# Last attention of a two-block transformer kernel: outputs formed transposed in one PSUM bank, gates and softmax sums multiplied into the weights on GpSimd

## What is computed

```python
q = rmsnorm(proj[..., :1024].reshape(b, s, 16, 64), q_norm)
gate = sigmoid(proj[..., 1024:])                       # 3 gates per head
o_cmp = softmax(q @ k_cmp.T) @ v_cmp                   # 15 compressed keys
o_sel = softmax(masked(q @ k_sel.T)) @ v_sel
o_win = softmax(masked(q @ k_win.T)) @ v_win
out = gate0 * o_cmp + gate1 * o_sel + gate2 * o_win
h = h + out.reshape(b, s, 1024) @ w_o
```

## Time and profile before

| | |
|---|---|
| median of three runs | 1619.47 us (1617.98 to 1620.32) |
| the profiled execution, its own time | 1619.05 us |
| its span, first to last instruction | 1616.0 us |
| PE busy | 1600.5 us, 99% of the span |
| DVE busy | 1033.2 us, 64% |
| ACT busy | 802.4 us, 50% |
| POOL busy | 36.8 us, 2% |
| DMA | 291.21 MB, mean 180 GB/s |
| PE clock granted, mean | 1.000 |
| the chain that ended last | PE 91%, DVE 5%, ACT 2% |

### The profile page before, as it was taken

The page is one execution under the profiler, slowest core; times in us unless marked ns, Lnnn a source line. Parts: engine busy times, 40 slices in busy tenths (PEclk is TensorE's granted clock), DMA queues, the critical chain, the costliest instruction groups (busy, mean ns, idle before and its releaser), DMA issues.

```text
span 1616.0 us, 21201 instructions
## 1 busy us (share of the span) xinstructions
PE 1600.5 (99%) x8796; PEld 1375.2 (85%) x8796; DVE 1033.2 (64%) x1223; ACT 802.4 (50%) x1091; POOL 36.8 (2%) x53
## 2 busy tenths in 40 slices
PE   8999999999999999999999999999999999999999
PEld 6888898877888888888899888889888887888887
DVE  5666556887766747666457666557666557766662
ACT  5555254765355534554344555446555445555551
POOL 0000000000000000000000000001000011000000
PEclk9999999999999999999999999999999999999999
DMA  9665574435476546555464665557565551056652
GB/s 289 186 228 184 170 261 137 144 117 176 141 224 212 218 147 217 183 198 201 162 219 156 204 191 196 196 173 247 168 193 200 187 195 53 11 172 195 197 182 78
DMA packets 226559, 291.21 MB, mean 180 GB/s; under 512 B 10596, under 2 KB 203808, under 8 KB 226336
## 3 DMA queue, kind: packets, MB, share of 16 engines
q1 hardware_dynamic: 226464, 289.87, 54.6%
HBM read 288.78 MB, written 1.05 MB: 179 GB/s over the span
## 4 chain that ended last, share of the span: by engine, by line
PE 91%; DVE 5%; ACT 2%; SPq 1%; issue 1%; DMA 1%; POOL 0%; DVEq 0%
PE bank L2003 24%; PE bank L2008 12%; PE bank L1813 9%; PE bank L1818 9%; PE bank L1822 9%; PE bank L1901 5%; PE bank L1888 5%; PE bank L1893 5%; PE bank L1862 2%; PE bank L1869 2%; DVE w_lo L1125 2%; PE bank L1864 2%; PE bank L2380 1%; PE bank L1789 1%; DMA raw<-in_ffn_w_up_dram 1%
## 5 line engine op out<-in xcount | busy, mean ns | idle before, releaser
L1125 DVE TENSOR_TENSOR w_lo<-raw,w_hi 128x2048 fp32r<-128x2048 f32 (+1 forms) x267 | 599.7, 2271 | 172.9 <-ACT w_hi L710 171.9
L710 ACT ACTIVATE w_hi<-raw 128x2048 fp32r<-128x2048 f32 (+1 forms) x267 | 506.6, 1904 | 167.4 <-DMA raw<-in_ffn_w_down_dram 93.4
L2003 PE MATMUL bank<-xT,w_hi 128*128 128x512 f32 x1664 | 397.3, 391 | 0.0
L2003 PEld LDWEIGHTS bank<-xT,w_hi 128*128 128x128 f32 x1664 | 306.1, 188 | 59.5
L2008 PEld LDWEIGHTS bank<-xT,w_lo 128*128 128x128 f32 x1664 | 213.3, 191 | 8.1
L2008 PE MATMUL bank<-xT,w_lo 128*128 128x256 f32 x1664 | 215.9, 283 | 0.0
L1072 ACT ACTIVATE silu<-bank 128x256 f32<-128x256 f32 x104 | 34.2, 381 | 215.9 <-PE bank L2008 215.9
L1818 PE MATMUL bank<-w_hi,hT_lo 128*128 128x512 f32 x528 | 134.9, 390 | 0.0
L1813 PE MATMUL bank<-w_hi,hT_hi 128*128 128x512 f32 x528 | 133.8, 389 | 0.0
L1822 PE MATMUL bank<-w_lo,hT_hi 128*128 128x512 f32 x528 | 133.7, 389 | 0.0
L1888 PE MATMUL bank<-w_hi,xT 128*128 128x512 f32 (+2 forms) x456 | 119.3, 392 | 0.0
(11 more groups left out here) (290 smaller groups left out, 1584.3 us busy)
## 6 DMA issues: line engine op xcount, KB each, us to landing
raw<-in_ffn_w_gate_up_dram SPq DMA_DIRECT2D x176, 512.0 KB, 4.8
raw<-in_ffn_w_down_dram SPq DMA_DIRECT2D x132, 512.0 KB, 4.0
raw<-in_w_in_dram SPq DMA_DIRECT2D x44, 512.0 KB, 4.9
raw<-in_ffn_w_gate_dram SPq DMA_DIRECT2D x43, 512.0 KB, 4.0
raw<-in_ffn_w_up_dram SPq DMA_DIRECT2D x43, 512.0 KB, 5.0
raw<-in_conv_w_in_dram SPq DMA_DIRECT2D x24, 512.0 KB, 4.6
raw<-in_kv_w_dram SPq DMA_DIRECT2D x12, 512.0 KB, 4.2
raw<-in_w_out_dram SPq DMA_DIRECT2D x8, 512.0 KB, 3.9
```

The source lines that it names most:

```text
L710: nc.scalar.activation(w_hi[:, slot, 0:width], raw[:, slot, 0:width], ACT.Copy).then_inc(high_ready, 1)
L1125: nc.vector.tensor_tensor(w_lo[:, slot, 0:width], raw[:, slot, 0:width], w_hi[:, slot, 0:width].bitcast(F32), ALU.subtract).then_inc(low_r ...
L2003: nc.tensor.matmul(o[:], hi[:, c, at], x, start=kh == 0 and c == 0, stop=False, skip_group_check=True)
```

## The change

**Scores.** A unit's banks are divided otherwise (`HEADS_AT`): bank 0 holds two tt = 1 heads, banks 1 and 2 one tt = 1 head and two tt = 0 heads each. The four 256-column matmuls come first, then the four of 128 columns, always one of each partition half in turn. Each bank signals for itself: `sel_scored`, `sel_least`, `sel_exped`, `sel_weighed`, `sel_scaled` and `selT_psum` count three per unit. The queries carry the factor -1/8, so minima replace maxima and the small negation goes.

**Coefficients.** `weigh` takes the banks one by one: three reciprocals and three products per unit in place of one each. GpSimd first copies the gates into a table by unit (`unit_gate`, eight copies), and then multiplies each head's weights in `sel_p` by its coefficient, eight tensor_scalar operations per unit. The transposes now wait for that (`sel_scaled`).

**Outputs.** The values are stationary (64 columns wide), the weights move: nine f32 matmuls per unit, of 256 or 128 columns, whose result has the features on partitions. The two heads of a pair write the two partition halves of a bank. The selected, the window and the compressed branch of a chunk add up in one bank (6 or 7 in turn), and ACT and DVE take `xT_hi` and `xT_lo` straight from it (`attended_chunks`). `add_unit`, `add_compressed` and the 16 transposes of `z_sb` go.

**Order.** The first w_o slab is interleaved with the last unit's transposes and outputs (`opening`). On DVE `weigh` moves ahead of the copy for unit 0, and from unit 3 on minima and `weigh` alternate by banks around the split of a weight slab.

```diff
-        SCORES = [[3, 4, 5], [0, 1, 2]]
+        SCORES = [[4, 2, 3], [5, 0, 1]]
+        CMP_TURNED = 7
+        HEADS_AT = [[(1, 0), (1, 3)], [(1, 1), (0, 0), (0, 1)], [(1, 2), (0, 2), (0, 3)]]
-        SCORE_ORDER = [(0, 0), (1, 2), (0, 1), (1, 3), (0, 2), (1, 0), (0, 3), (1, 1)]
+        SCORE_ORDER = [(1, 0), (1, 2), (1, 1), (1, 3), (0, 0), (0, 2), (0, 1), (0, 3)]
```

On GpSimd, behind the query roots:

```diff
+                    pool.wait_ge(branch_gates, 1)
+                    for b in range(3):
+                        for k, (tt, i) in enumerate(HEADS_AT[b]):
...
+                            ins = pool.tensor_copy(to, src[:, :, :, 1:3, i // 2, i % 2])
+                    ins.then_inc(unit_gates, 1)
+                    for w in range(UNITS):
+                        for b in range(3):
+                            pool.wait_ge(sel_weighed, 3 * w + b + 1)
+                            for k, head in enumerate(HEADS_AT[b]):
+                                p, c = sel_p[:, w % 2, b, score_place(*head)[1]], FIRST_AT[b] + k
+                                ins = pool.tensor_scalar(p, p, sel_coef[:, w % 2, c:c + 1], None, ALU.mult)
+                            ins.then_inc(sel_scaled, 1)
```

On ACT:

```diff
+                    for w in range(2, UNITS):
+                        if w + 1 < UNITS:
+                            exponentials(w + 1, range(0, 1))
+                        turned_weights(w)
+                        if w == 2:
+                            compressed_weights(0)
                         if w == 3:
+                            compressed_weights(1)
+                        if w + 1 < UNITS:
+                            exponentials(w + 1, range(1, 3))
+                        if w == 2:
                             split_to(s0 + 7)
-                        transposed_weights(w)
-                    evacuate_input(inputs_before(n) + 1, HALVES_FIRST)
+                        if w >= 3 and w != 5:
+                            attended_chunks({3: 0, 4: 1, 6: 2, 7: 3}[w])
```

On DVE:

```diff
-                    row_maxima(1)
-                    transposed_weights(0)
+                    row_minima(1)
                     weigh(0)
+                    turned_weights(0)
...
                     masked(0)
-                    row_maxima(2)
-                    transposed_weights(1)
+                    row_minima(2)
+                    weigh(1)
                     masked(1)
+                    turned_weights(1)
...
-                    weigh(1)
-                    add_unit(0)
+                    weigh(2)
+                    row_minima(3)
...
                     for w in range(3, UNITS):
...
+                        turned_weights(w)
+                        if w + 1 < UNITS:
+                            weigh(w + 1, range(0, 1))
                         if w <= 5:
                             split_to(s0 + w + 2)
...
+                        if w != 5:
+                            attended_chunks({3: 0, 4: 1, 6: 2, 7: 3}[w])
+                        if w + 1 < UNITS:
+                            weigh(w + 1, range(1, 2))
+                            if w + 2 < UNITS:
+                                row_minima(w + 2, range(0, 1))
+                            weigh(w + 1, range(2, 3))
+                            if w + 2 < UNITS:
+                                row_minima(w + 2, range(1, 3))
```

On PE:

```diff
                     def transpose_weights(w):
-                        pe.wait_ge(sel_exped, w + 1)
                         for b in range(3):
-                            for i in range(4):
...
-                        ins.then_inc(selT_psum, 1)
+                            pe.wait_ge(sel_scaled, 3 * w + b + 1)
+                            for to, i in enumerate(TURNED_FROM[b]):
+                                ins = nc.tensor.transpose(bank[SCORES[w % 2][b]][:, to * P:(to + 1) * P], sel_p[:, w % 2, b, i * P:(i + 1) * P], ident[:])
+                            ins.then_inc(selT_psum, 1)
...
-                        for tt in range(NT):
-                            for r in range(PER_GROUP):
...
-                                    ins = nc.tensor.matmul(o, p, values[:, key_tile, g * HD:(g + 1) * HD], start=key_tile == 0, stop=key_tile == tt)
+                        weighted(0, 0, every, 3)
+                        weighted(1, 0, every, 0)
+                        weighted(0, 1, second, 5)
+                        weighted(1, 1, second, 2)
+                        weighted(2, 0, every, 9)
+                        weighted(3, 0, first, 8)
+                        weighted(3, 0, second, 7)
+                        weighted(2, 1, second, 11)
+                        weighted(3, 1, second, 6).then_inc(sel_out, 1)
...
+                    def opening(part):
+                        pe.wait_ge(xT_ready, first_input + 2)
+                        part(0, [0])
+                        transpose_weights(7)
+                        part(1, [0], between=last_units)
+                        pe.wait_ge(xT_ready, first_input + 4)
+                        part(0, [1], True).then_inc(slab_used, 1)
```

More of the change, by code:

```diff
@@ L1826, in project @@
                 first = slabs - tail(n)
-                for d in range(first):
+                if opening:
+                    opening(part)
+                for d in range(0 if not opening else first, first):
                     ready(d)
@@ L1838, in project @@
                 for tt in range(NT):
-                    for d in range(first, slabs):
+                    for d in range(first + 1 if opening and tt == 0 else first, slabs):
                         between = None
@@ new lines, in outputs @@
+                        every, first, second = slice(0, S), slice(0, P), slice(P, S)
+                        weighted(0, 0, every, 3)
[7 more added lines that the diff above has]
+                        weighted(3, 1, second, 6).then_inc(sel_out, 1)
@@ L2441, in _ @@
[L2441 to L2447 removed]
+                    transpose_weights(4)
```

297 lines of the change are left out of this document (133 added, 164 removed).

## The result

The changed kernel takes 1647.2 us (median of 4 runs, 1645.87 to 1648.97), the kernel before on the same chip 1618.72 (1617.6 to 1620.32): 1.0176 times as long, 95% interval 1.0158 to 1.0193. The forecast was 1622.0 with a range to 1631; it is outside. The profiled execution took 1648.97 us, its span 1647.1. Four executions of the kernels in this document (1758 to 3206 us) were in a slower state of the chip and are left out of all medians.

What follows compares the result with a forecast made beforehand. PE, busy 99% at full clock, was taken as the bound. Four attention stretches and shorter scores summed -0.3 + 8.1 - 2.5 + 0.8 - 4.0 = +2.1 us, plus 1 for `weigh`'s product: 1619.05 + 3 = 1622.0 us, range 1616 to 1631.

Steps and rivals of the forecast that it cites:

- the assumed prices: GpSimd's scaling passes: 0.94 us for bank 0 and 1.19 us each for banks 1 and 2 of a unit.
- the dear passes: Rival: GpSimd's scaling passes take 4 to 4.7 us a unit, giving +6 to +9.5 us; chance 0.17.
- 3.3 us a unit: GpSimd's eight scaling passes of a unit, priced from rows of other operations; bounds 2.8 and 4.7 us.
- full clock: Forecast case: PE's clock stays full, GpSimd 2.8 to 3.8 us a unit, time +0 to +5.5 us; chance 0.50.
- The clock rival: Rival: PE idles about 3 us twice in the attention and its clock falls, +4 to +7 us more; chance 0.23.
- stretch A: Attention from unit 1's scores to the end of unit 1's transposes: 17.7 us for 9.6 before, +8.1.
- B: Attention from there to the end of unit 4's transposes: 24.9 us for 27.4 before, -2.5.
- C: Two rounds of the attention's rhythm: 14.4 us together for 13.6 before, +0.8.
- the ring of C: Chain of `weigh`, GpSimd, transposes, copies, slab split and reduction: 7.0 us one round, 7.2 to 7.4 the second.
- D: Rest of the attention: 7.8 us for 10.9 before plus 0.9 of transposes inside the projection, -4.0.
- 1 us for the small product in `weigh`: DVE's two-input product waits for a GpSimd pass, 0.4 us at most, in about five units: 1 us more.
- scores 1.5: A unit's eight score matmuls, equal sizes side by side: 1.5 us in place of 1.84, 2.7 us saved in all.

Runs made afterwards that it cites:

- the waits filled: Changed kernel with dummy matmuls in all of PE's waits for GpSimd: 1638.5 us; with GpSimd passes cut to 80 and 40 columns and dummy matmuls: 1623.6 us.
- constant factor: Changed kernel with GpSimd multiplying by the constant 0.5 in place of the coefficient column: 1641.8 us.
- short passes: Changed kernel with GpSimd multiplying only 80 of each 256 columns and 40 of each 128: 1632.2 us.
- one product: Changed kernel with GpSimd scaling by products of two tiles, five instructions a unit in place of eight: 1632.5 us.
- shared in the written order: Changed kernel with bank 0 of each unit scaled by GpSimd, banks 1 and 2 by DVE, order unchanged: 1628.0 us.
- new order: Changed kernel, passes still on GpSimd, with compressed scores ahead of the first transposes and `weigh` ahead of the next unit's reductions for units 0 and 1: 1637.2 us.
- short passes, filled: Changed kernel with GpSimd passes cut to 80 and 40 columns and dummy matmuls in PE's waits: 1623.6 us.
- new order, DVE: Changed kernel with scaling passes on DVE, compressed scores ahead of the first transposes and `weigh` ahead of the next unit's reductions for units 0 and 1: 1621.7 us.

## Why the prediction was wrong

The sum of the loss in medians: 28.5 us = 4.1 (the written order with the assumed prices, most of it) + 15.0 (1623.6 to 1638.5: the dear passes, both with the waits filled) + 8.7 (1638.5 to 1647.2: the clock), with 0.7 between the runs of before. Without filling, the dear passes cost the same 15.0 (1632.2 to 1647.2) and at the assumed prices the clock costs the same 8.7 (1623.6 to 1632.2), so the two shares do not depend on which is taken first. The 4.1 still holds up to 1.7 of lost clock.

- **Failed: "3.3 us a unit" for GpSimd's passes, upper bound 4.7.** It is 5.95, outside the bounds. The nearest rows were affine selects and a cast to bf16 (the 291 ns for 128 columns), other operations of the engine; that they bound a `tensor_scalar` was assumed. The upper bound's 0.17 us for fetching the coefficient stood on no row; the constant factor puts it at 0.08. A longer distance between row and operation should have given a wider bound. The Trainium skill (GPSIMD Engine Reference, "4.1 Engine selection") puts one-input elementwise work on GpSimd at roughly the full rate and two-input work at about half of VectorE's. The traces disagree on the first (0.90 us against DVE's 0.27 for 256 columns) and have the product of two tiles cheaper than the one-input form.
- **Failed: "full clock" as the forecast's case, and rivals taken one at a time.** The clock rival had 0.23 and +4 to +7; it came true with 8, and on top of the dear passes. It also came true at the assumed prices (short passes, 1632.2). The prediction had the waits of about 3 us, and in every kernel here that has them ahead of the first transposes (3.87 us, 2.99 with short passes, 3.05 with one product, 3.90 shared in the written order) the clock fell. The rule of the Trainium skill (TensorE: Matmul & The Clock Gate, "HAM oscillation — how this bites in real kernels") that was cited for this rival is borne out in kind; the places are the stretches of 0.50 behind the 3.87 and 3.44 us. The runs go beyond it: the clock also fell behind waits under 1 us, and once with no wait at all.
- **Right: stretch A's mechanism.** `weigh(0)` behind all reductions of unit 1 leaves PE idle 3.87 us (forecast: about 3), the same again for unit 1; its 17.7 became 27.4 by the price and the clock. With the assumed price and the waits filled it is 19.7. Taking the order away (new order) gives back 10 us.
- **B and C** (24.9 and 14.4, measured 32.2 and 20.5): the ring of C was right with its price 3.3 (14.44 measured with short passes, filled); with 5.95 GpSimd takes most of the ring (15.88 busy of 20.52 us), and half-speed outputs (2.43 and 2.76 us) add to it. The exclusion by a split is as forecast (3.80 us for two passes).
- **D** (7.8, measured 9.9): the outputs of unit 5 and the compressed pair behind them still ran at half clock (0.88 over the stretch).
- **Failed, small: 1 us for the small product in `weigh`.** It was counted as waiting for GpSimd's passes. It did not: the 16 of 128x3 take 170 ns as a mean, and the one at 1350.95 took 0.16 us with a pass running since 1350.93. So the exclusion shows in one direction only for these passes, the split holding up GpSimd. With products on GpSimd it shows in both. Why the forms differ is open.

```profile
L1634 DVE TENSOR_TENSOR sel_coef<-sel_coef,unit_gate 128x3 f32<-128x3 f32 x16 | 2.7, 170 | 0.5
```

- **Right: outputs 1.5 us a unit** (1.46), and the gate copies at no cost (1.1 us in all, less than the 2.1 forecast).
- **Failed, small: "scores 1.5"** (1.82, no gain over 1.84). In the windows of line 2357 alone (length, PE, weight loads) the last 0.84 us hold eight weight loads, those of the four 128-column scores: 0.105 us a record, one behind the other, where the 256-column ones need 0.98 for eight.

```profile
1389.37:1390.35 0.98, 0.98 (x8) 0.90 (x10) 1.00 0.08 17
1390.35:1391.19 0.84, 0.84 (x11) 0.72 (x8) 1.00 0.00 0
```

- **"PE's work falls by about 14 us. The change is worth that only if PE does not wait"**: right in kind. By the measured prices it falls by about 12 (8 x 1.22 for outputs, 8 x 0.02 for scores, 1.8 for the transposes). Where PE hardly waits, 7 to 10 us of it come out by the medians, 9 to 12 by the rest.

## What to carry to other kernels

A bound for an operation that the trace does not show is worth what the likeness of its rows is worth; on GpSimd, time the instruction form itself, since two forms of the same multiplication differed by 0.90 to 0.57 us. A wait of about 3 us ahead of short PE work is priced with the clock behind it, and this comes on top of what makes the wait; several short waits around short work are to be priced so too, since they lost the clock here as well. And when work leaves one engine but lengthens a chain, write the orders of all engines anew for that chain: here kernels that scale with products on GpSimd cost 12 us in the old order and gained 7 in a new one.

## What the runs showed of the hardware

- GpSimd's f32 `tensor_scalar` in place: 0.90 us for 256 columns, 0.58 for 128, 0.46 for 80, 0.35 for 40: 0.26 us and 2.5 ns a column. Constant factor 0.82 and 0.49. Product of two tiles 0.57 for 256 and 1.04 for 512. DVE's `tensor_scalar` 0.27 and 0.20.
- A slab split on DVE held up a GpSimd pass (two passes in 3.80 us for 1.8) and a GpSimd product of 512 columns (3.02 for 1.04). A GpSimd product held up DVE's small product (0.98 for 0.16); GpSimd's `tensor_scalar` passes did not (170 ns as a mean).
- The granted clock fell to half behind PE waits of 3.87, 3.44, 2.99 and 2.94 us, in rounds with waits of 0.9 and 1.9 us around a few transposes, behind waits of 0.53, 0.94 and 0.88 us, and once (new order, DVE, at 1350 us) with PE busy throughout; it did not fall behind one of 2.81 us between stretches of full work. What decides between them is left open.
- The work that pays for a wait is what stands behind it, not the waiting work alone: the outputs, which wait for nobody here, took 2.29 us in place of 1.46.
